# Two-block transformer on one core: columns spread by transposes in place of fp32 products, reciprocals written wide

## The chip, the cores and the metric

The kernel runs on one core of one Trainium2 chip (trn2). The metric is the device time of one execution in microseconds. One execution was also taken by the hardware profiler; all rows below come from it.

## The reference

Two transformer blocks follow each other on x (1, 512, 1024), all in fp32. Only what matters for the change is shown.

```python
def rms_norm(x, gain):
    y = xf * lax.rsqrt(jnp.mean(xf * xf, axis=-1, keepdims=True) + NORM_EPS)
    return (y * gain.astype(jnp.float32)).astype(x.dtype)

def first_block(x, c, ...):
    cond = jax.nn.silu(c)
    for i in range(DEPTH):                       # 2 layers
        mod = (cond @ ada_w[i] + ada_b[i]).reshape(b_, N_SUBLAYERS, 3, D_MODEL)
        h = adaln(x, norm_g[i, 0], mod[:, 0, 0], mod[:, 0, 1])
        x = x + 0.5 * (1.0 + mod[:, 0, 2]) * swiglu(h, ...)
        # mixer: pooling in layer 0, fox_attention (16 heads of 64) in layer 1
        # a second swiglu with its own adaln
def second_block(x, ...):
    # layer 0: hybrid attention. Heads 0-7 attend through masks that count three dilations;
    # 4 more head pairs are differential: softmax 1 minus lam * softmax 2, then an rms norm
    # layer 1: gated linear recurrence; each layer ends with a convolutional feed-forward
```

In both attentions every softmax row is divided by its sum.

## The kernel before

**Layout.** X, HH and HL hold activations with the 1024 channels on the partitions, as 8 tiles of 128 x 512 tokens. All large products are fp32 made of three fp32r products: each weight chunk of 128 x 1024 (raw) is loaded by SyncE, split by ScalarE into a high part wh (L543) and by VectorE into a low part wl (L998), and TensorE multiplies wh by the high and low parts of the activation and wl by the high part (L1732, L1921, L1786 to L1789). Four chunks are in the ring. Each engine has one fixed order of work, written by hand; semaphores join them. The two PSUM halves PS[0] and PS[1] have four banks each.

**Norms.** There are ten (six adaln in the first block, four in the second). VectorE adds squares per tile, `square_sums` (L1812) sums them over the partitions, so that the mean square stands as a column of tokens: st4[:, 1, a] holds the roots of 128 tokens. `spread_root` (L1851 to L1860) turns a column into a row and repeats it on all partitions: an fp32 product of the column, stretched to 128x128 by a broadcast, with the identity. The product shows as two records. Nine norms make two calls (one per half of the tokens) with two products each, the first norm makes one call with four. The calls stand between the large products: in `tilewise` behind the 11th block of the second half, in `halved_units` behind the third tile, in the pooling stage and at the start. `h_scale` on VectorE (L1152) waits for rb_ready, which the call signals. `keep_busy` (L1803) runs five bf16 products behind the first call.

**Condition.** At the start (L2018) eight such products spread silu(c) over PS[1]; VectorE copies the result to condb (L1341), against which it multiplies the rows of ada_w (L1068). Then TensorE transposes x (L2027).

**Attention.** Both attentions go by pairs of heads, 8 pairs each. For pair i the steps are: `score_mms` (L1935), on VectorE `pair_scores` (L1277: score plus bias, with the row minimum as a by-product), on ScalarE `pair_exp` (L658, with the sums Z[:, slot, qt]), on VectorE `pair_sums` (L1282 to L1295, reciprocal into rz), `transposes` of the probabilities (L1987, 20 blocks in five rounds through banks 4, 5, 6, 7, 4), `turned_copies` by ScalarE (L670) and VectorE (L1306), `value_mms` (L1940 to L1967), and the multiplication by the spread reciprocals (L1548) into OT; then the split of the result into HH (ScalarE L849) and HL (VectorE L1573). The stages of three pairs overlap: in iteration i of the loop TensorE makes the scores of pair i, the values of pair i-2 and the transposes of pair i-1. Third round of the transposes: it waits for pv_read of the pair before, which L1548 signals, because both use bank 6.

Only "plain" pairs spread their reciprocals: all 8 pairs of the first attention (fox) and the last 4 of the second (i >= COMBINED = 4), twelve in all. `value_mms` makes 8 products (L1950), four blocks of tokens times two heads, each with 64 stretched columns, into bank 7; ScalarE copies that to OT (L836). In the differential pairs (the first 4 of the second attention) L1289 to L1295 combine the two heads instead, and L1552 and L1561 scale.

The order on VectorE in iteration i of the first attention is: scores of rounds 0 and 1 of pair i, pair_sums of pair i-1, L1548 of pair i-2, scores of round 2, three copies L1306, L1573. On ScalarE: exponentials of round 0, L836, exponentials of round 1, L670 twice with the exponentials of round 2 behind, L849. pair_exp waits for rz_ready of the pair two before (its Z slot), value_mms for rz_ready of its own pair. QB holds the queries; tile i of it is read by score_mms of pair i alone.

Of the kernel before, what the change touches and what calls it, by code (L numbers as in the profile page):

```python
# [179 lines left out]
def build(nc, A, out, upto=None):  # L180
    plan, NCH = make_plan(upto)
    ctx = ExitStack()
    with ctx:
# [32 lines left out]
        ident = sb("ident", [128, 128])  # L216
# [7 lines left out]
        st4 = sb("st4", [128, 6, 4])  # L224
# [4 lines left out]
        Z = sb("Z", [128, 4, 4])  # L229
        rz = sb("rz", [128, 4, 4])  # L230
# [3 lines left out]
        QB = arena[:, 0:4096].rearrange("p (k t) -> p k t", k=KT)  # L234
# [44 lines left out]
        PS = [ctx.enter_context(nc.psum_tensor(f"PS{i}", [128, 4, 512], F32)) for i in range(2)]  # L279

        def plain(fox, i):

            return fox or i >= COMBINED

        def tile_of(fox, i):

            return i if fox else SECOND[i]
# [6 lines left out]
        def t_rounds(fox, i):  # L294

            if i == 0:
                return T_AHEAD[fox]
            return T_FIRST if fox else T_PLAIN if plain(fox, i) else T_COMBINED

        def attend_bank(b, g):  # L300

            return PS[(g + b // 4) % 2][:, b % 4, :]
# [47 lines left out]
        bias_masked, rz_ready, combined, sub_summed, rz_spread, rz_copied = (sem(n) for n in (  # L350
            "bias_masked", "rz_ready", "combined", "sub_summed", "rz_spread", "rz_copied"))
# [35 lines left out]
        def P(name, i=0, n=1):  # L387
            c = COL[name] + i
            return par[:, c:c + n]
# [594 lines left out]
        def _(dve):  # L984
# [297 lines left out]
            def pair_sums(pair, i, fox):  # L1282

                slot = 2 * (pair % 2)
                dve.wait_ge(p_ready, 8 * pair + 8)
                if plain(fox, i):
                    nc.vector.reciprocal(rz[:, slot:slot + 2, :], Z[:, slot:slot + 2, :]).then_inc(rz_ready, 1)
                    return
                link(nc.vector.reciprocal(rz[:, slot:slot + 2, :], Z[:, slot:slot + 2, :]))  # L1289
                link(TS(rz[:, slot + 1, :], rz[:, slot + 1, :], lam[:, 5:6], None, ALU.mult))  # L1290
                TT(rz[:, slot + 1, :], rz[:, slot + 1, :], Z[:, slot, :], ALU.mult).then_inc(rz_ready, 1)
                dve.wait_ge(rz_ready, pair + 1)
                for qt in (3, 2, 1, 0):
                    first, second = (SP_[:, slot + u, SEG[qt]:SEG[qt + 1]] for u in range(2))
                    STT(first, second, rz[:, slot + 1, qt:qt + 1], first, ALU.mult, ALU.add).then_inc(combined, 1)  # L1295
# [38 lines left out]
            for st in plan:  # L1334
                kind, c, g = st["kind"], st["c"], st["g"]
# [59 lines left out]
                elif kind == "ffn":  # L1395
# [4 lines left out]
                    for ng, nt in st["halves"]:  # L1400
                        if ada:
                            paired = st is plan[2] and c == st["c"]
                            if paired:
# [5 lines left out]
                                e, cv, g, c, j = e + 2, cv + 2, g + 2, c + 8, j + 2  # L1409
                            for u in range(2 if paired else 0, ng):  # L1410
# [5 lines left out]
                                e, cv, g, c, j = e + 1, cv + 1, g + 1, c + 4, j + 1  # L1416
# [11 lines left out]
                        e, cv, g, c, j = e + 2 * pairs, cv + 2 * pairs, g + 2 * pairs, c + 8 * pairs, j + 2 * pairs  # L1428
                        if ng % 2 and not ada:
                            split_until(c + 4 + RING)  # L1430
                            hidden_group(st, e, g, cv, j, 4 * pairs, 0)
                            e, cv, g, c, j = e + 1, cv + 1, g + 1, c + 4, j + 1
# [36 lines left out]
                elif kind == "attproj":  # L1469
                    for i in range(4):  # L1470
                        c += 4
                        if st["fox"] and i == 0:
# [7 lines left out]
                            m, p, mn = accf[0:HEADS, 5120:5632], SG[0:HEADS, 0, :], PR[0:HEADS, 0, :]  # L1480
# [13 lines left out]
                        q = st["q"] + i  # L1494
# [5 lines left out]
                        for p in range(2):  # L1500
# [4 lines left out]
                            y, t = PR[:, :, :], WK[:, 2 * p:2 * p + 2, :]  # L1505
# [12 lines left out]
                    pair, fox = st["a"] // 2, st["fox"]  # L1518
# [13 lines left out]
                elif kind == "attend":  # L1532
                    p0, fox = st["a"] // 2, st["fox"]
                    for i in range(2, PAIRS + 2):
# [10 lines left out]
                        if plain(fox, i - 2):  # L1545
                            o = OT_flat(b)
# [147 lines left out]
                elif kind == "finish":  # L1694
                    for a in range(4):
                        dve.wait_ge(out_act, a + 1)
                        dve.wait_ge(tile_done, st["td"] + a + 1)
                        o = XOUT[:, a, 512:D]
# [4 lines left out]
        def _(pe):  # L1703
            MM = nc.tensor.matmul
# [146 lines left out]
            def spread_root(nm, h):  # L1851


                ps, halves = PS[nm["g"] % 2], (h,) if nm["n"] else (0, 1)
                pe.wait_ge(root_ready, norm_at(nm, h))
                for a in (a for half in halves for a in (2 * half, 2 * half + 1)):
                    o = 128 * (a % 2)
                    mm = MM(ps[:, 2 + a // 2, o:o + 128], st4[:, 1, a:a + 1].broadcast_to((128, 128)), ident[:, :],
                            start=True, stop=True, skip_group_check=True)
                mm.then_inc(rb_ready, 1)  # L1860

            def turn_back(g, half):
# [77 lines left out]
            def value_mms(pair, i, fox, g):  # L1940

                bank, slot, col = attend_bank(6, g), 2 * (pair % 2), 128 * tile_of(fox, i)
                pe.wait_ge(pt_act, before(pair + 1, 2, 2))
                if plain(fox, i):
                    pe.wait_ge(rz_ready, pair + 1)
                    if not fox:
                        pe.wait_ge(pt_vec, before(pair, 3, 1) + 2)
                    for qt in range(4):
                        for u in range(2):
                            mm = MM(attend_bank(7, g)[64 * u:64 * u + 64, 128 * qt:128 * qt + 128],  # L1950
                                    rz[:, slot + u, qt:qt + 1].broadcast_to((128, 64)), ident[:, :],
                                    start=True, stop=True, skip_group_check=True)
                    mm.then_inc(rz_spread, 1)
                pe.wait_ge(pt_vec, before(pair + 1, 3, 1))
                if plain(fox, i):
                    for kt in range(4):
                        for u in range(2):
                            at_, n = 10 * u + KT_AT[kt], 4 - kt
                            mm = MM(bank[64 * u:64 * u + 64, 128 * kt:512], VB[:, kt, col + 64 * u:col + 64 * u + 64],
                               PTS[:, at_:at_ + n, :].rearrange("p n q -> p (n q)"), start=(kt == 0), stop=(kt == 3),  # L1960
                               skip_group_check=True)
                else:
                    for qt in range(4):
                        for kt in range(qt + 1):
                            mm = MM(bank[:, 128 * qt:128 * qt + 128], PTS[:, KT_AT[kt] + qt - kt, :], VB[:, kt, col:col + 128],
                                    start=(kt == 0), stop=(kt == qt), skip_group_check=True)
                mm.then_inc(pv_done, 1)  # L1967
# [41 lines left out]
            for st in plan:  # L2009
                kind, c, g, n = st["kind"], st["c"], st["g"], st["n"]  # L2010
                h_ready_at = lambda k: [(h_ready, st["h"] - KT + k + 1)]
                nm = plan[plan.index(st) - 1] if kind in ("ffn", "attproj", "rec", "poolmix") else None
                if kind == "start":
                    pe.wait_ge(ident_in, 16)
                    pe.wait_ge(cond_act, 1)
                    for i in range(KT):
                        o = 128 * (i % 4)
                        mm = MM(PS[1][:, 2 + i // 4, o:o + 128], P("cond", i).broadcast_to((128, 128)), ident[:, :],  # L2018
                                start=True, stop=True, skip_group_check=True)
                    mm.then_inc(cond_wide, 1)  # L2020
                    for k in range(KT):
                        if k % 4 == 0:
# [14 lines left out]
                elif kind == "ffn":  # L2037
                    e = st["e"]
                    c_last = c + sum(4 * ng + nt for ng, nt in st["halves"])
                    for ng, nt in st["halves"]:  # L2040
                        pairs, e2 = ng // 2, e
                        if nm:
# [5 lines left out]
                            c, g, e2, pairs, nm = c + 8, g + 2, e2 + 2, pairs - 1, None  # L2048
# [7 lines left out]
                        for half in range(2):  # L2056
# [6 lines left out]
                            c, g = c + nt // 2, g + 1  # L2063
# [331 lines left out]
```

## Time and profile before

| | us |
|---|---|
| median of 3 runs | 2970.56 (2969.76 to 2972.46) |
| profiled execution, its time | 2972.09 |
| profiled execution, its span | 2970.2 |
| TensorE busy | 2934.7, 99% |
| VectorE busy | 1648.1, 55% |
| ScalarE busy | 1144.9, 39% |
| GpSimd busy | 145.5, 5% |

The span goes from the first to the last instruction. Matmul ends are modelled by the profiler; the starts of successive records tell how long a group holds TensorE. An idle time in brackets at the end of a timeline row is that of the engine before the instruction, with the instruction that ended it.

### The profile page before, as it was taken

The page shows a single profiled execution, that of the slowest core. Times are in us where ns is not written, and L with a number is a line of the kernel's source. Part 1 is how long each engine was busy: PE and PEld are TensorE (multiplying, and loading weights), DVE is VectorE, ACT ScalarE, POOL GpSimd, SP SyncE. Part 2 cuts the span into 40 slices and gives each one's busy share as a digit, 9 for nine tenths or more (in the row PEclk, how much of TensorE's full clock was granted, in tenths as well). Part 3 has the DMA queues.
Part 4 walks back from the last instruction along what each step waited for, and adds up shares of the span by engine and source line. Part 5 has one row for each costly group of instructions (what it writes and reads, how often), then busy time and mean ns, then how long its engine had stood idle before and what let it go on. Part 6 is the DMA issues. An engine that isn't in the chain of part 4 may idle for free. (4 is left out here: it accounts for less than half of the span.)

```text
span 2970.2 us, 37552 instructions
## 1 busy us (share of the span) xinstructions
PE 2934.7 (99%) x14365; PEld 2443.0 (82%) x14365; DVE 1648.1 (55%) x2338; ACT 1144.9 (39%) x1586; POOL 145.5 (5%) x297
## 2 busy tenths in 40 slices
PE   9999989999999999999999999999999999999999
PEld 7888888888888888868888888768888888888887
DVE  7747476444653336875433357766535557754453
ACT  4223253222432225464332234554423338443242
POOL 0101001000010001040000000110000001000000
PEclk9999999999999999999999999999999999999999
DMA  7837326554362322241322223422322322323222
GB/s 295 275 127 262 121 73 227 175 163 149 123 218 93 99 99 97 92 168 68 114 94 98 99 74 100 141 88 86 101 98 92 100 92 79 107 85 106 92 99 71
DMA packets 100914, 366.56 MB, mean 123 GB/s; under 512 B 11248, under 2 KB 11808, under 8 KB 100784
## 3 DMA queue, kind: packets, MB, share of 16 engines
q1 hardware_dynamic: 77616, 276.56, 27.4%
q0 software_dynamic: 23168, 88.17, 8.8%
q8 instruction: 93, 1.52, 0.2%
q14 instruction: 37, 0.30, 0.0%
HBM read 362.51 MB, written 2.18 MB: 123 GB/s over the span
## 5 line engine op out<-in xcount | busy, mean ns | idle before, releaser
L998 DVE TENSOR_TENSOR wl<-raw,wh 128x1024 fp32r<-128x1024 f32 x501 | 609.2, 1225 | 971.9 <-ACT wh L543 971.8
L543 ACT ACTIVATE wh<-raw 128x1024 fp32r<-128x1024 f32 x501 | 524.1, 1056 | 1205.4 <-PE PS L1732 1148.7
L1732 PE MATMUL PS<-HH,wh 128*128 128x512 f32 x2432 | 947.6, 390 | 4.8 <-DVE HL L1580 3.2
L1732 PE MATMUL PS<-HL,wh 128*128 128x512 f32 x2432 | 947.0, 389 | 0.0
L1732 PE MATMUL PS<-HH,wl 128*128 128x512 f32 x2432 | 946.6, 389 | 0.0
L1732 PEld LDWEIGHTS PS<-HH,wh 128*128 128x128 f32 x2432 | 456.8, 188 | 101.9 <-DVE HL L1580 4.3
L1732 PEld LDWEIGHTS PS<-HH,wl 128*128 128x128 f32 x2432 | 456.9, 188 | 95.1
L1732 PEld LDWEIGHTS PS<-HL,wh 128*128 128x128 f32 x2432 | 456.9, 188 | 94.3
L1732 PE MATMUL PS<-AH,wh 128*128 128x512 f32 x848 | 330.1, 389 | 0.5 <-DVEq L1615 0.5
L1732 PE MATMUL PS<-AH,wl 128*128 128x512 f32 x848 | 329.9, 389 | 0.0
L1732 PE MATMUL PS<-AL,wh 128*128 128x512 f32 x848 | 329.9, 389 | 0.0
L1732 PEld LDWEIGHTS PS<-AH,wh 128*128 128x128 f32 x848 | 159.2, 188 | 34.3 <-DVEq L1615 0.9
L1732 PEld LDWEIGHTS PS<-AH,wl 128*128 128x128 f32 x848 | 159.2, 188 | 33.0
L1732 PEld LDWEIGHTS PS<-AL,wh 128*128 128x128 f32 x848 | 159.2, 188 | 33.0
L1332 DVE TENSOR_TENSOR AL<-PR,AH 128x1024 fp32r<-128x1024 f32 (+1 forms) x68 | 83.3, 1226 | 87.4 <-ACT AH L694 87.4
L1322 DVE SCALAR_TENSOR_TENSOR WK<-PS,par,WK 128x511 f32<-128x511 f32 (+1 forms) x192 | 128.1, 740 | 0.0
L694 ACT ACTIVATE AH<-PR 128x1024 f32 (+1 forms) x68 | 72.1, 1061 | 137.3 <-DVE PR L1313 103.5
L1068 DVE CUSTOM_DVE_ANT_0 acc<-acc 128x1024 f32<-128x1024 f32 x86 | 104.1, 1219 | 5.1 <-DMA acc<-in_stream 5.0
L1921 PE MATMUL PS<-AH,wh 128*128 128x256 f32 (+1 forms) x312 | 100.1, 321 | 0.0
L1921 PE MATMUL PS<-AL,wh 128*128 128x256 f32 (+1 forms) x312 | 99.3, 318 | 0.0
L1921 PE MATMUL PS<-AH,wl 128*128 128x256 f32 (+1 forms) x312 | 99.3, 318 | 0.0
L658 ACT ACTIVATE acc<-acc,NM 128x128 f32<-128x128 f32 (+3 forms) x128 | 70.5, 553 | 32.6 <-DVE NM L1277 32.5
(278 smaller groups left out, 3117.7 us busy)
## 6 DMA issues: line engine op xcount, KB each, us to landing
raw<-in_stream SPq DMA_DIRECT2D x501, 512.0 KB, 3.3
acc<-in_stream POOLq DMA_DIRECT2D x86, 512.0 KB, 4.8
piece<-in_stream POOLq DMA_DIRECT2D x42, 512.0 KB, 4.8
arena<-in_stream SPq DMA_DIRECT2D x16, 512.0 KB, 12.5
TBa<-negcum POOLq DMA_DIRECT2D x8, 640.0 KB, 5.1
TBa<-in_alibi POOLq DMA_DIRECT2D x8, 640.0 KB, 4.7
TBb<-negcum POOLq DMA_DIRECT2D x4, 640.0 KB, 4.9
piece<-negcum POOLq DMA_DIRECT2D x4, 640.0 KB, 6.0
```

The source lines that it names most:

```text
L543: F(wh[:, r, :], raw[:, r, :], ACT.Copy).then_inc(hi_done, 1)
L658: F(seg, seg, ACT.Exp, bias=NM[:, slot, qt:qt + 1], scale=-1.0, accum_out=Z[:, slot, qt:qt + 1]).then_inc(p_ready, 1)
L694: F(dst, PR[:, :, :], ACT.Copy).then_inc(act_hi, 1)
L998: TT(wl[:, r, :], raw[:, r, :], wh[:, r, :].bitcast(F32), ALU.subtract).then_inc(lo_done, 1)
L1068: return nc.vector.tensor_tensor_reduce(tile, tile, condb, 1.0, 0.0, ALU.mult, ALU.add, mod[:, s, j:j + 1])
L1322: ins = STT(y, PS[g % 2][:, t, 0:S - sh], w, y, ALU.mult, ALU.add)
L1332: TT(dst, PR[:, :, :], hi.bitcast(F32), ALU.subtract).then_inc(a_ready, 1)
L1732: mm = MM(PS[g % 2][:, j, :], l, x, start=(first and i == 0), stop=(last and i == 2), skip_group_check=after_halves)
L1921: mm = MM(PS[g % 2][:, t, cols(h)], l, x, start=(k == 0 and i == 0), stop=(k == nt - 1 and i == 2), skip_group_check=True)
```

## The change

Three places that spread a column by an fp32 product with the identity now do it by a transpose of the same stretched column: spread_root, the condition, and the reciprocals in value_mms. For the last, the eight products of 64 columns become four transposes of 128: the reciprocals of a pair are first written out stretched. VectorE's reciprocal in pair_sums of a plain pair reads the 8 sums of a token 64 times each and writes 128x512 into tile tile_of(fox, i) of QB, the query tile that the pair no longer needs, where it wrote 128x8 into rz. Semaphores and their counts stay as they are, and so does the order of instructions on every engine. Differential pairs are untouched.

```diff
+        def rz_wide(fox, i):
+            return QB[:, tile_of(fox, i), :]
@@ pair_sums (VectorE)
                 if plain(fox, i):
-                    nc.vector.reciprocal(rz[:, slot:slot + 2, :], Z[:, slot:slot + 2, :]).then_inc(rz_ready, 1)
+                    nc.vector.reciprocal(rz_wide(fox, i).rearrange("p (q u f) -> p u q f", q=4, u=2),
+                                         Z[:, slot:slot + 2, :].unsqueeze(3).broadcast_to((128, 2, 4, 64)))\
+                        .then_inc(rz_ready, 1)
                     return
@@ spread_root (TensorE)
                     o = 128 * (a % 2)
-                    mm = MM(ps[:, 2 + a // 2, o:o + 128], st4[:, 1, a:a + 1].broadcast_to((128, 128)), ident[:, :],
-                            start=True, stop=True, skip_group_check=True)
+                    mm = nc.tensor.transpose(ps[:, 2 + a // 2, o:o + 128], st4[:, 1, a:a + 1].broadcast_to((128, 128)),
+                                             ident[:, :])
@@ value_mms (TensorE)
                     for qt in range(4):
-                        for u in range(2):
-                            mm = MM(attend_bank(7, g)[64 * u:64 * u + 64, 128 * qt:128 * qt + 128],
-                                    rz[:, slot + u, qt:qt + 1].broadcast_to((128, 64)), ident[:, :],
-                                    start=True, stop=True, skip_group_check=True)
+                        t = slice(128 * qt, 128 * qt + 128)
+                        mm = nc.tensor.transpose(attend_bank(7, g)[:, t], rz_wide(fox, i)[:, t], ident[:, :])
@@ start (TensorE)
                         o = 128 * (i % 4)
-                        mm = MM(PS[1][:, 2 + i // 4, o:o + 128], P("cond", i).broadcast_to((128, 128)), ident[:, :],
-                                start=True, stop=True, skip_group_check=True)
+                        mm = nc.tensor.transpose(PS[1][:, 2 + i // 4, o:o + 128], P("cond", i).broadcast_to((128, 128)),
+                                                 ident[:, :])
```

## Rows read from the trace of the kernel before

**Rows 1.** The page: span, and busy time, share and instructions of each engine.

```profile
span 2970.2 us, 37552 instructions
PE 2934.7 (99%) x14365; PEld 2443.0 (82%) x14365; DVE 1648.1 (55%) x2338; ACT 1144.9 (39%) x1586; POOL 145.5 (5%) x297
```

**Rows 2.** Busy time by windows, both attentions; columns: stretch, length, engines, PEclk, DMA.

```profile
1290.00:1320.00 30.00, 30.00 (x240) 20.81 (x239) 22.80 (x69) 21.15 (x59) 14.52 (x31) 1.00 0.45 150
...
1920.00:1950.00 30.00, 25.48 (x172) 17.15 (x171) 23.44 (x79) 23.99 (x95) 14.64 (x54) 0.95 0.48 170
```

**Rows 3.** Instructions of one line: count, ns min/median/max, starts, shape.

```profile
L1858 PE MATMUL PS<-ident,st x80: 270/275/421, 13.3 to 2574.7; 128*128 128x128 f32 x80
...
L1950 PE MATMUL PS<-ident,rz x192: 272/273/323, 1298.2 to 1973.3; 128*64 128x128 f32 x192
```

**Rows 4.** Timeline of TensorE around one root call; columns: start us, us, what.

```profile
1138.70 0.28 PE L1921 MATMUL PS<-AH,wl 128*128 128x256 f32 x1
...
1138.82 0.60 PE L1858 MATMUL PS<-ident,st 128*128 128x128 f32 x4
...
1139.18 0.36 PE L1921 MATMUL PS<-AH,wh 128*128 128x256 f32 x1
```

**Rows 5.** Timeline of TensorE: 20 transposes and the product behind them.

```profile
1291.24 2.34 PE L1987 MATMUL PS<-ident,acc 128*128 128x128 f32 x20
...
1293.35 0.48 PE L1732 MATMUL PS<-wh,HH 128*128 128x512 f32 x1
```

**Rows 6.** VectorE's groups by line and shape: count, busy us, mean ns, idle before.

```profile
L1306 DVE COPY PTS<-PS 128x512 f32<-128x512 f32 x36 | 23.4, 687 | 5.6 <-PE PS L1987 4.9
...
L1516 DVE COPY arena<-PS 128x2048 f32<-128x2048 f32 x2 | 4.6, 2283 | 0.0
...
L1287 DVE RECIPROCAL rz<-Z 128x8 f32<-128x8 f32 x12 | 2.4, 197 | 0.0
...
L1044 DVE TENSOR_SCALAR gains<-par 128x1 f32<-128x1 f32 x7 | 0.5, 145 | 0.0
...
L1230 DVE TENSOR_TENSOR mod<-mod,par 128x8 f32<-128x8 f32 x1 | 0.2, 168 | 0.0
```

**Rows 7.** Timeline of all engines: a round of the first attention, the next reciprocal.

```profile
1304.01 0.60 ACT L670 ACTIVATE PTS<-PS 128x512 f32<-128x512 f32 x1 [0.65 <-PE PS L1987]
...
1305.49 0.62 ACT L849 ACTIVATE HH<-acc 128x512 fp32r<-128x512 f32 x1
...
1306.13 0.69 DVE L1573 TENSOR_TENSOR HL<-acc,HH 128x512 fp32r<-128x512 f32 x1 [1.00 <-ACT HH L849]
...
1306.27 1.09 PE L1950 MATMUL PS<-ident,rz 128*64 128x128 f32 x16
...
1306.74 0.28 DVE L1277 CUSTOM_DVE_ANT_0 acc<-PS,TBa 128x128 f32<-128x128 f32 x1
...
1307.19 2.32 PE L1959 MATMUL PS<-PTS,arena 128*64 128x512 f32 x16
...
1309.34 0.20 DVE L1287 RECIPROCAL rz<-Z 128x8 f32<-128x8 f32 x1
...
1309.83 0.69 DVE L1548 TENSOR_TENSOR acc<-PS,acc 128x512 f32<-128x512 f32 x1 [0.28 <-ACT acc L836]
...
1317.41 0.20 DVE L1287 RECIPROCAL rz<-Z 128x8 f32<-128x8 f32 x1
```

**Rows 8.** Timeline of VectorE in the second attention: reciprocal and what follows.

```profile
1943.12 0.20 DVE L1287 RECIPROCAL rz<-Z 128x8 f32<-128x8 f32 x1
1943.67 0.69 DVE L1552 TENSOR_TENSOR acc<-PS,rz 128x512 f32<-128x512 f32 x1 [0.35 <-PE PS L1965]
...
1969.47 0.69 DVE L1548 TENSOR_TENSOR acc<-PS,acc 128x512 f32<-128x512 f32 x1 [1.13 <-PE PS L1959]
```

**Rows 9.** The start: the condition's line, and a window (columns as in rows 2).

```profile
L2018 PE MATMUL PS<-ident,par x16: 421/421/580, 3.4 to 6.7; 128*128 128x128 f32 x16
...
19.00:21.00 2.00, 2.00 (x6) 1.54 (x6) 2.00 (x4) 0.23 (x1) 0.00 (x0) 0.50 1.03 412
```

## The prediction

> **What bounds the kernel now.** I read the page first: over a span of 2970.2 us TensorE is busy 99% of the time, VectorE 55% [rows 1]. So a microsecond taken from TensorE is normally a microsecond of the result, and one given to VectorE normally costs nothing. That average must not be used for the two attention stages, so next I read the table by windows. In 30 us of the first attention TensorE is busy 30.0, VectorE 22.8 and ScalarE 21.2 us; in 30 us of the second TensorE falls to 25.5, and the granted clock there to 0.95 [rows 2]. There three engines hand one pair of heads round, and a slower VectorE can set the pace. The third view is the timeline of one round, the fourth the groups by line and shape.
>
> **Part 1, the roots (spread_root, L1858).** One fp32 product shows as two records: 40 products, 80 records [rows 3]. A call in the middle of the stream makes two products; its four records hold TensorE from 1138.82 to 1139.18, 0.36 us [rows 4]. An fp32 transpose is one record: 20 of them take 1291.24 to 1293.35, 0.105 us each [rows 5]. Two take 0.21, so a call saves 0.15 us. There are 18 such calls, two in each of nine norms, nearly all of them with TensorE work back to back on both sides: **2.7 us saved**. The reader of the root, VectorE's L1152, gets it 0.15 us sooner as well, and no transfer hangs on it. A transpose that reads one column 128 times is not in the trace. From below it can't cost less than the 0.09 us of one product record [rows 4], from above the two records that it replaces; I take 0.105, the ordinary transpose, because its row has the same shape and type. Bounds 0 to 3.2 us saved.
>
> **Part 2, the condition (L2018).** Eight products, 16 records, run before x has landed, and the first transposes of x wait for that DMA anyway, so the saving is worth nothing. Their records take 421 ns where the same shape later takes 270 to 275: TensorE runs at half speed there although the granted clock reads 1.00 [rows 3, 9]. Half as many records leave TensorE idle before x lands, so the 32 transposes of x can stay at the slow pace longer. At worst they take about 3 us more; part of this is covered, because the root, which is spread behind them, comes from VectorE later than they end. The stretch from 19 to 21 us runs at a granted 0.50 (1.2 GHz) [rows 9]; such a fall of about 3.4 us costs 1.7 us and can move or double. I take +0.5 us, bounds -1.5 to +4.
>
> The Trainium skill, page "TensorE: Matmul & The Clock Gate", Part 4, says that transpose mode doesn't count as busy for the clock. By that rule products turned into transposes make falls of the clock likelier, at 1.7 us each as above. The trace does not bear it out in the first attention, where half of the instructions are transposes and the clock stays at 1.00 [rows 2].
>
> **Part 3, the products of the reciprocals (L1950).** Eight products with 64 columns each, 16 records, from 1306.27 to the next group's 1307.19, 0.92 us [rows 7]; four full transposes take 0.42 [rows 5], with a changeover 0.5. It saves 0.4 us a pair, twelve pairs, **if TensorE sets the pace there**.
>
> **Part 4, the reciprocal (L1287).** It wrote 8 elements a partition and now writes 512, on VectorE, in order, ahead of L1548. This decides the case. An 8-element reciprocal takes 197 ns. An 8-element product of two tensors takes 168. Copies take 687 ns for 512 elements and 2283 for 2048: 1.04 ns an element on a base of 155 [rows 6]. Two readings of 197 are possible. Either the reciprocal has a longer start and then runs at 1.04 ns an element: 512 elements take 0.72 us. Or each element takes longer: (197 - 168) / 8 + 1.04 = 4.7 ns, or on the copies' base (197 - 155) / 8 = 5.2 ns, or on the base of a one-element operation, 145 [rows 6], 6.5 ns. That makes 2.6, 2.8 or 3.5 us for 512. A division in several steps is the more natural reading of a row that stands 17% above another operation of its size, and I take 2.8 us, on the copies' base, since a reciprocal has one operand like them. Ends: 0.72 and 3.5 us.
>
> The Trainium skill, page "VectorE: DVE Perf Modes", the walkthrough's hardware budget, describes the reciprocal as an iterative divide with a repeat count of 8. Eight steps of 1.04 ns would be 4.4 us for 512 elements. The same rule gives 222 ns for 8 elements, and the row has 197, so in size the trace agrees only in part.
>
> Now the place. In a round of the first attention the order on VectorE is L1573, six score reductions, reciprocal, L1548, two more reductions, three copies. The rounds are 8.07 us apart (1309.34 and 1317.41), and from the reciprocal's start to L1548's are 0.49 us, the last 0.28 waiting for ScalarE's L836 [rows 7]. An instruction starts some 0.08 us before the end of the one ahead of it (L1573 takes 0.69, the next starts after 0.61 [rows 7]), so a reciprocal of 2.8 moves L1548 to 2.72 us behind its start, 2.23 later. What follows L1548 today takes 3.68 us until L1573. It starts with the third round of transposes, which waits for L1548 to free its bank, then ScalarE's copy L670, two exponentials and L849 [rows 7]. With TensorE waiting at that bank this part shrinks to 8 x 0.105 for two rounds of transposes + 0.28 for the end of the last record [rows 3] + 0.5 + 1.0 (together 1304.01 to 1305.49) + 0.64 for L849 and the start behind it = 3.3 us. The round becomes 3.3 + 0.61 + 2.60 + 2.72 + 0.69 = 9.9 us, **1.85 us longer**, and TensorE has over 2 us of idle in it, so that part 3 is worth nothing. Five rounds: 9.25. In the first round the cover is 0.99, +1.73; in the last with a reciprocal 1.21, +1.51. Pair 0's reciprocal stands among weight splits with free time on all engines: 0. In the second attention four reciprocals are wide; L1552 or L1548 starts 0.55, 1.30, 1.31 and 1.33 us behind them (the first stands whole in [rows 8], of the last its idle time; the covers of the rounds not shown, six in all, are read in the same way), so +2.17, +1.42, +1.41 and +1.39. Together **18.9 us**. Each 0.1 us on the reciprocal moves it by 1.1 us: 16.5 with 2.6 us and 26.6 with 3.5. I know of no wait that moves: the bank of L1950 and ScalarE's first exponential wait for a reciprocal that is a whole round old.
>
> The gaps of 2 us in TensorE invite falls of the clock inside the attentions. Most of a fall is hidden by those same gaps; one that runs into the dense products behind costs 1.7 us. I take +1, bounds 0 to 5.
>
> **Sum.** -2.7 + 0.5 + 0 + 18.9 + 1.0 = +17.7 us. The profiled execution has a span of 2970.2 and took 2972.1, so 1.9 lie around the span; its time after is 2989.8. It stands 1.5 above the median of 2970.56, so the prediction is 2988.3, **2988 us**, +0.6%.
>
> **Rivals.** (a) *The reciprocal only has a longer start*, 0.72 us. Then L1548 comes 0.15 us later than today at most, the pace stays TensorE's, and part 3 counts: about 0.3 us in each of eleven rounds, 3.3 us, and 2.7 from the roots: -6, 2965 us. This is the other side. It decides as long as the reciprocal's start-to-start time stays under about 0.9 us, the cover it has in a round; for it speaks that a single size can't tell start from rate. (b) *Eight steps an element*, 4.4 us: 11 x 1.6 = 17.6 us more than my sum, 3006 us; against it speaks the 197 ns. That is the price of the page's rule, worked out from the copies' 1.04 ns. (c) *The reciprocal is iterative but half as slow, about 1.7 us*, part start and part rate: 18.9 - 12.1 = 6.8, in all +5.6, 2976 us. (d) The change would not do what it says if stretched columns slowed the transposes to the price of products: part 1 goes, 2.7 us more than the sum; inside the range.
>
> **How the numbers follow.** Chances: forecast with 2.6 to 3.5 us a reciprocal 0.63 (its own range 2981 to 2998), (a) 0.13, (b) 0.19, (c) 0.05. The range 2975 to 3008 takes in (b) and (c) and leaves (a) out. A measurement of this kernel can tell about 0.2%, 6 us. Slower by more is the forecast, (b) and a part of (c): 0.85. Within 0.2%: half of (a), the rest of (c): 0.08. Faster: half of (a): 0.07.
>
> **What would show it.** The row of the wide reciprocal, 128x512, at 2.6 to 3.5 us is the step on which all rests; at 0.7 rival (a) has won. The time from one such row to the next in the first attention should be 9.9 instead of 8.07 us; TensorE's transposes should wait for L1548, some 2 us a round. The root's call should take 0.21 us instead of 0.36, with half as many records. The number of stretches at 0.50 should rise by no more than three. The prediction is wrong if the reciprocal's rate is wrong, or if the second attention hides more than its covers say.

## The result and the profile after

The change made the kernel slower, by the mechanism that was forecast and by a little more than the forecast size:

| | before | after |
|---|---|---|
| median of 5 runs, us | 2972.03 | 2995.69 |
| lowest to highest, us | 2969.76 to 2972.70 | 2992.21 to 2996.92 |
| profiled execution: time, span, us | 2972.1, 2970.2 | 2995.9, 2994.0 |
| mean granted clock | 0.997 | 0.994 |

The ratio of after to before is 1.0076, with a 95% interval of 1.0065 to 1.0086. The forecast was 2988, with a range of 2975 to 3008. (The 2970.56 that it starts from is the median of the first three of the five runs before.)

In the code after the change the line numbers are higher by 4 to 6: the reciprocal is L1291 (was L1287), the accumulation behind it L1554 (L1548), the turning transposes L1991 (L1987), the copies behind them L674 and L1312 (L670, L1306), the spread of the reciprocals L1956 (L1950), that of the roots L1864 (L1858), the split behind the round L1579 (L1573).

The page after, which answers to [rows 1]:

```profile
span 2994.0 us, 37168 instructions
PE 2934.9 (98%) x14173; PEld 2437.1 (81%) x14173; DVE 1683.1 (56%) x2338; ACT 1144.6 (38%) x1586; POOL 144.1 (5%) x297
```

TensorE has 192 records fewer and is busy for the same 2935 us; VectorE has as many instructions as before and is busy for 35.0 us more. Twelve rows account for all of it and a little more. VectorE's groups by line and shape (count, busy us, mean ns, idle before), beside which [rows 6] has 12 at 197 ns:

```profile
L1291 DVE RECIPROCAL arena<-Z 128x512 f32<-128x512 f32 x12 | 40.2, 3348 | 0.0
L1295 DVE RECIPROCAL rz<-Z 128x8 f32<-128x8 f32 x4 | 0.8, 198 | 0.0
```

Twelve reciprocals grew from 2.4 to 40.2 us, 37.8 more. The span grew by 23.8. So most of the time added to an engine that is busy 56% of the span became time of the kernel. The waits of TensorE say how (who waited, for whom: us in total, times, longest):

```profile
PE PS L1991 <- DVE acc L1554: 19.3, 10, 2.4
PE PS L1991 <- DVE acc L1558: 3.1, 4, 0.9
```

The transposes at L1991 want the bank that L1554 reads, and L1554 stands behind the reciprocal on VectorE. One round of the first attention, from the timeline of all engines (start us, us, what, and in brackets the idle time and what ended it), to be laid beside [rows 7]:

```profile
1299.74 3.35 DVE L1291 RECIPROCAL arena<-Z 128x512 f32<-128x512 f32 x1
...
1303.01 0.63 DVE L1554 TENSOR_TENSOR acc<-PS,acc 128x512 f32<-128x512 f32 x1
...
1303.69 1.53 PE L1991 MATMUL PS<-ident,acc 128*128 128x128 f32 x12 [1.64 <-DVE acc L1554]
...
1306.94 0.69 DVE L1579 TENSOR_TENSOR HL<-acc,HH 128x512 fp32r<-128x512 f32 x1 [0.83 <-ACT HH L853]
...
1307.55 0.28 DVE L1281 CUSTOM_DVE_ANT_0 acc<-PS,TBa 128x128 f32<-128x128 f32 x1
...
1310.15 3.35 DVE L1291 RECIPROCAL arena<-Z 128x512 f32<-128x512 f32 x1
...
1313.42 0.63 DVE L1554 TENSOR_TENSOR acc<-PS,acc 128x512 f32<-128x512 f32 x1
...
1314.10 2.15 PE L1991 MATMUL PS<-ident,acc 128*128 128x128 f32 x12 [2.40 <-DVE acc L1554]
```

From one reciprocal to the next are 10.41 us, where [rows 7] have 8.07. The round can be added up from these rows: 3.27 from the reciprocal's start to L1554's, 0.63 for L1554, 3.30 from its end to L1579, 0.61 until the score reductions begin, 2.60 for these. That is 10.41.

Where the 23.8 us arose, from the starts of the same instructions in both traces:

| stretch | before, us | after, us | difference |
|---|---|---|---|
| start to the first reciprocal | 1283.65 | 1282.21 | -1.4 |
| first attention, to its last L1554 (before: L1548) | 70.50 | 88.79 | +18.3 |
| on to the first reciprocal of the second attention | 545.62 | 544.69 | -0.9 |
| second attention, to its last L1554 | 75.96 | 85.28 | +9.3 |
| on to the end of the span | 994.5 | 993.0 | -1.4 |

### The profile page after: what moved, and what is told of

Same layout as the page of the kernel before. It is cut to its first block and busy times, and to the rows that moved or that the text cites. A ratio compares the mean times of both kernels' runs of the same rounds, so it can differ in the third digit from the quotient of the medians.

```text
span 2994.0 us, 37168 instructions
## 1 busy us (share of the span) xinstructions
PE 2934.9 (98%) x14173; PEld 2437.1 (81%) x14173; DVE 1683.1 (56%) x2338; ACT 1144.6 (38%) x1586; POOL 144.1 (5%) x297
## 6 DMA issues: line engine op xcount, KB each, us to landing
arena<-in_stream SPq DMA_DIRECT2D x16, 512.0 KB, 12.6
```

## The experiments

Each kernel ran beside the kernel before. In this table the ratio to before has its 95% interval behind it; the change is in us against the runs of before that go with it.

| kernel | median, us | ratio | against before |
|---|---|---|---|
| the change | 2995.69 | 1.0076 (1.0065 to 1.0086) | +23.7 |
| roots and condition only | 2969.28 | 0.9989 (0.9980 to 0.9998) | -3.3 |
| roots only | 2968.84 | 0.9986 (0.9977 to 0.9995) | -3.7 |
| wide reciprocal and its transposes only | 2996.91 | 1.0082 (1.0067 to 1.0098) | +24.4 |
| half of the wide reciprocal | 2973.20 | 1.0003 (0.9993 to 1.0012) | +1.1 |
| wide reciprocal, products kept | 2992.59 | 1.0071 (1.0057 to 1.0085) | +20.7 |
| wide reciprocal later in the round | 3002.75 | 1.0101 (1.0086 to 1.0117) | +30.6 |
| small reciprocal, VectorE spreads it | 2966.34 | 0.9978 (0.9968 to 0.9987) | -6.2 |
| the same, later in the round | 2967.68 | 0.9985 (0.9976 to 0.9994) | -4.4 |
| small reciprocal, ScalarE spreads it | 2967.47 | 0.9984 (0.9975 to 0.9993) | -4.7 |

**The parts alone.** The first kernel is the one before with the transposes for roots and condition, the second has them for the roots alone, the third is the change with both put back:

```diff
-                    mm = MM(ps[:, 2 + a // 2, o:o + 128], st4[:, 1, a:a + 1].broadcast_to((128, 128)), ident[:, :],
-                            start=True, stop=True, skip_group_check=True)
+                    mm = nc.tensor.transpose(ps[:, 2 + a // 2, o:o + 128], st4[:, 1, a:a + 1].broadcast_to((128, 128)),
+                                             ident[:, :])
```

> Only the roots and the condition are spread by transposes; the attentions are as before. Theory A (the changed kernel's trace: a call holds TensorE 0.13 us, from 1137.73 to 1137.86, against 0.36 before): 18 calls x 0.23 = 4.1 us less, the start about 0.2 us later, so 3.9 us less than before. Theory B (the recorded sum, 0.105 us a transpose): 2.7 us less. Theory C (it does nothing, time is lost again in waits): 0.

> Only the roots are spread by transposes. Theory A (the condition's products are hidden behind the load of x): the same time as with the condition changed too, within 0.5 us, so 4.1 us less than before. Rival (fewer records at the start leave TensorE slow for longer): 0.5 to 4 us less time than with both changed.

> Only the wide reciprocals with their transposes; roots and condition as before. Theory A (all of the loss comes from the 3.35 us reciprocal ahead of the product with the spread reciprocals): about 27.6 us more than before, 18.3 in the first attention and 9.3 in the second. Rival (part of the loss comes from the start or the roots): less than 26 us more.

Measured: -3.3 us for roots and condition, -3.7 us for the roots alone, so the condition gives and takes nothing that can be seen. Theories A (3.9) and B (2.7) of the first kernel can't be told apart by its 3.3; the row of the root call, shown further below, does that. For the wide reciprocal with its transposes it is +24.4 us, where theory A had 27.6 and the rival less than 26. So theory A missed by 3, but not for the rival's reason: by the same five stretches as in the table above, this kernel differs from the one before by -0.6, +15.6, 0.0, +8.9 and -0.7 us, and all of its loss, 24.5 us, is in the attentions. What it lacks of the 27.6 is 2.7 us in the first attention, and there its trace differs from the change's in the clock. Its rounds are all 10.41 us; the change has two of 10.88 and 11.29, and a last stretch that is 1.3 us longer, each with a fall of the clock in it (an interval at the lower level, 0.50 of full speed). Over the same 30 us, the change first and then this kernel (stretch, length, engines, granted clock, DMA):

```profile
1290.00:1320.00 30.00, 25.96 (x165) 16.91 (x165) 25.34 (x58) 18.10 (x51) 9.62 (x21) 0.94 0.41 146
1290.00:1320.00 30.00, 25.96 (x173) 16.79 (x173) 25.05 (x56) 18.61 (x53) 10.98 (x22) 1.00 0.39 134
```

The parts add up roughly: 24.4 - 3.3 = 21.1, beside the 23.7 measured. The intervals reach 3 to 5 us either way, and the 2.7 us of the clock are about the difference. The loss is in the attentions, where parts 3 and 4 are, and the small gain in part 1; the products put back, below, part 3 from 4.

**The size of the reciprocal.** Half of it, 256 elements in place of 512:

```diff
-                    nc.vector.reciprocal(rz_wide(fox, i).rearrange("p (q u f) -> p u q f", q=4, u=2),
-                                         Z[:, slot:slot + 2, :].unsqueeze(3).broadcast_to((128, 2, 4, 64)))\
+                    nc.vector.reciprocal(rz_wide(fox, i)[:, 0:256].rearrange("p (q u f) -> p u q f", q=2, u=2),
+                                         Z[:, slot:slot + 2, 0:2].unsqueeze(3).broadcast_to((128, 2, 2, 64)))\
```

> The changed kernel with the wide reciprocal over the first two of four token blocks alone (128x256); the reciprocals of the other two blocks are left out, so their results are not the reference's. Theory A (the cost is a rate, 6.25 ns an element, and a round of the attention lengthens by what the reciprocal takes beyond its cover): the row takes 0.147 + 256 x 6.25 = 1.75 us, 1.6 less than in the changed kernel, and eleven rounds give back 17 to 18 us: about 10 us above the kernel with narrow reciprocals and copy, 2976 to 2979. Rival (a long start that grows little with size): the row stays above 2.5 us and the time above 2985.

Measured: 2973.2 us, 22.5 below the change. VectorE's group and, in the fence behind it, TensorE's wait in this kernel:

```profile
L1291 DVE RECIPROCAL arena<-Z 128x256 f32<-128x256 f32 x12 | 21.0, 1748 | 0.0
```

```profile
PE PS L1991 <- DVE acc L1554: 5.0, 9, 0.8
```

The row is as expected, 1.75 us. With it the sum of a round is 1.67 + 0.63 + 3.30 + 0.61 + 2.60 = 8.81 us, and all five rounds of the first attention are 8.81 us apart in the trace. The reciprocal is then 1.6 us shorter, and the kernel 22.5 us: 11 x 1.6 is 17.6. The time undercut the expected 2976 to 2979 by 2.8 us or more. Most of the rest is the clock: in the first attention this kernel keeps 1.00, the change has 0.95. Its attentions take 74.28 and 78.12 us. Beside the kernel with the wide reciprocal and its transposes alone, whose rounds in the first attention no fall of the clock lengthened (86.10 and 84.82 us), the half size gives back 11.8 + 6.7 = 18.5 us, near the 17.6; beside the change itself 14.5 + 7.2 = 21.7.

**The products put back.** The wide reciprocal stays, the eight products of 64 columns return:

```diff
-                        t = slice(128 * qt, 128 * qt + 128)
-                        mm = nc.tensor.transpose(attend_bank(7, g)[:, t], rz_wide(fox, i)[:, t], ident[:, :])
+                        for u in range(2):
+                            o = 128 * qt + 64 * u
+                            mm = MM(attend_bank(7, g)[64 * u:64 * u + 64, 128 * qt:128 * qt + 128],
+                                    rz_wide(fox, i)[:, o:o + 64], ident[:, :],
+                                    start=True, stop=True, skip_group_check=True)
```

> The changed kernel with its wide reciprocal and its roots, but the eight fp32 products of 64 columns a pair back in place of the four transposes; they read the wide columns, so everything that is computed is the reference's. It measures part 3 alone, while VectorE sets the pace. My step 'part 3 is worth nothing once the reciprocal is wide' expects the time of the changed kernel, 2995.7 us within 1.5, rounds of the first attention of 10.4 us as there, and TensorE's wait at L1991 for VectorE's L1554 shorter by about the 0.5 us a round that the products take longer. Rival: TensorE's work in a round still counts in full, 0.4 to 0.5 us in each of eleven rounds, about 5 us more, 3000 to 3001 us.

Measured: 2992.6 us (2991.8 to 2994.6). The median is 3.1 below the change, the runs overlap with the change's 2992.2 to 2996.9, and it is nowhere near 3000; but the expected 2995.7 within 1.5 was missed too, on the fast side. Its wait (L1991 is L1994 here), and two reciprocals of its timeline:

```profile
PE PS L1994 <- DVE acc L1554: 15.9, 10, 2.1
```

```profile
1298.35 3.35 DVE L1291 RECIPROCAL arena<-Z 128x512 f32<-128x512 f32 x1
1308.76 3.35 DVE L1291 RECIPROCAL arena<-Z 128x512 f32<-128x512 f32 x1
```

TensorE does more and waits 3.4 us less over ten waits. Three of the five rounds are 10.41 us as in the change; the two others, with a fall of the clock in them, are 10.57 and 10.95 where the change has 10.88 and 11.29. So in these rounds an instruction taken from TensorE only lengthens its wait: part 3 is worth nothing beside the wide reciprocal. That the median is even lower goes with the clock. By windows (stretch, length, engines, granted clock, DMA), first the change, then this kernel:

```profile
1270.00:1380.00 110.00, 94.39 (x556) 61.88 (x557) 86.19 (x184) 59.92 (x166) 31.84 (x70) 0.95 0.35 121
1900.00:2010.00 110.00, 93.94 (x546) 64.52 (x545) 83.41 (x206) 64.75 (x196) 20.11 (x70) 0.95 0.31 113
```

```profile
1270.00:1380.00 110.00, 97.00 (x658) 66.07 (x655) 85.36 (x182) 59.95 (x167) 32.32 (x70) 0.97 0.35 122
1900.00:2010.00 110.00, 94.64 (x597) 65.53 (x597) 80.36 (x204) 63.22 (x195) 19.14 (x68) 0.97 0.32 116
```

The time spent at 0.50 is twice what is missing to 1.00: 11 us in each attention of the change, 6.6 us here, 8.8 us less in all. At the level of 1.2 GHz the dense work takes double, so up to half of that, 4.4 us, is lost time. The spans of the two traces differ by 4.1 us: 1.7 in the first attention, 0.5 in the second, 1.4 ahead of the first reciprocal (in the first 30 us the change has a clock of 0.94, this kernel 1.00) and 0.5 behind the attentions. That is an accounting from one trace of each; no run holds the clock apart, and whether the products themselves keep it up is taken up below.

**The reciprocal's place.** The wide reciprocal moved behind the last scores of the round, ahead of the copies L1312 instead of ahead of L1554:

```diff
-                        if i <= PAIRS and plain(fox, i - 1):
-                            pair_sums(p0 + i - 1, i - 1, fox)
...
                             pair_scores(p0 + i, i, fox, g, (2,))
+                        if i <= PAIRS and plain(fox, i - 1):
+                            pair_sums(p0 + i - 1, i - 1, fox)
```

> The changed kernel with the full wide reciprocal, but behind the product with the spread reciprocals (L1554) and the scores of the last round, so ahead of the three copies. Theory A (with 3.3 us more a round VectorE has more work than a round is long, so the place gives back only its waits): the rounds become 9.7 us instead of 10.4 to 10.9, the time 4 to 8 us less than the changed kernel's, about 2990. Rival (only the place ahead of L1554, where TensorE waits for a bank, costs time): the rounds go back to 8.1 us and the time to about 2968.

Measured: 3002.8 us, 7 above the change, where 5 below was expected. This was a miss. TensorE's waits in this kernel, and behind them the longest in the timeline of the second attention:

```profile
PE PS L1991 <- DVE PTS L1312: 13.4, 4, 3.9
PE PS L1963 <- DVE PTS L1312: 7.1, 7, 1.0
PE PS L1956 <- DVE arena L1291: 5.0, 6, 2.3
```

```profile
1963.23 3.35 DVE L1291 RECIPROCAL arena<-Z 128x512 f32<-128x512 f32 x1
...
1967.69 1.28 DVE L1312 COPY PTS<-PS 128x512 f32<-128x512 f32 x2
...
1968.43 1.11 PE L1991 MATMUL PS<-ident,acc 128*128 128x128 f32 x4 [3.93 <-DVE PTS L1312]
```

L1554 is free now, and the next thing behind the reciprocal is late instead: the copies that empty the banks for the next transposes, by up to 3.9 us. In the first attention the rounds came down only from 10.41 to about 10.15, and the one behind them went from 7.8 up to 10.3; in the second they went from 9.1, 12.6, 11.4, 11.4 and 9.0 us to 10.3, 15.9, 15.0, 14.1 and 10.5. My reason had looked at one wait and not at what comes to stand behind the moved instruction. VectorE is the pace of the round, and at both places that were tried something that TensorE wants stands behind the reciprocal. The clock is not what makes the 7 us: three of the four executions took 3002.0 to 3003.1 us at a mean clock of 0.994, that of the change. The profiled one is the fourth, 3006.5 us at 0.992, so the rounds of its second attention, where the clock is 0.88, are somewhat too long for the median.

**A short way to the same columns.** The reciprocal of 8 elements as before, and a copy that repeats it into 512:

```diff
-                    nc.vector.reciprocal(rz_wide(fox, i).rearrange("p (q u f) -> p u q f", q=4, u=2),
-                                         Z[:, slot:slot + 2, :].unsqueeze(3).broadcast_to((128, 2, 4, 64)))\
+                    link(nc.vector.reciprocal(rz[:, slot:slot + 2, :], Z[:, slot:slot + 2, :]))
+                    nc.vector.tensor_copy(rz_wide(fox, i).rearrange("p (q u f) -> p u q f", q=4, u=2),
+                                          rz[:, slot:slot + 2, :].unsqueeze(3).broadcast_to((128, 2, 4, 64)))\
```

> The changed kernel, but VectorE takes the reciprocals of 8 elements (0.20 us) and then copies them stretched to 128x512. Theory A (it is the length of the reciprocal, 6.25 ns an element, not the writing of 512 elements or the transposes of QB): the copy takes 0.43 to 0.69 us, the product L1548 comes 0.2 to 0.4 us later than before in a round, the rounds are within 7.7 to 8.1 us, and the time is 4 to 7 us less than before. Rival (the wide write, the transposes from QB or the order cost the time): the rounds stay above 9 us and the kernel stays more than 10 us slower than before.

Measured: 2966.3 us, 6.2 below the kernel before and 29 below the change; the ratio's interval lies below 1, and this median is the lowest of all kernels here. Its groups on VectorE, and the same instructions in the timeline of one round:

```profile
L1292 DVE COPY arena<-rz 128x512 f32<-128x512 f32 x12 | 5.5, 460 | 0.4
L1291 DVE RECIPROCAL rz<-Z 128x8 f32<-128x8 f32 x12 | 2.4, 197 | 0.0
```

```profile
1307.16 0.20 DVE L1291 RECIPROCAL rz<-Z 128x8 f32<-128x8 f32 x1
1307.39 0.58 DVE L1292 COPY arena<-rz 128x512 f32<-128x512 f32 x1
1307.89 0.68 DVE L1555 TENSOR_TENSOR acc<-PS,acc 128x512 f32<-128x512 f32 x1
```

L1555 (the accumulation, one line further down here) starts 0.73 us behind the reciprocal, inside the 0.9 us of cover that the prediction found. TensorE is busy in all 30.0 us of the first attention's window again, at a clock of 1.00, and the rounds are 7.8 to 8.0 us behind a first of 8.55 (before: 8.07 behind 8.84). Parts 1 and 3 then both count: 3.3 to 3.7 for the roots, and 2.5 to 2.9 more for the transposes of the reciprocals. The stretches of the trace say the same: the first attention is 1.7 us shorter than before, the second 0.9. Four transposes hold TensorE for 0.59 us, from 1312.01 to 1312.60, where the products of [rows 7] hold it for 0.92:

```profile
1312.01 0.66 PE L1957 MATMUL PS<-ident,arena 128*128 128x128 f32 x4
1312.60 1.73 PE L1964 MATMUL PS<-PTS,arena 128*64 128x512 f32 x8
```

Two variants ask whether the spread can be made cheaper still: the same pair of instructions later in the round, as in the experiment on the place, and the copy on ScalarE, ahead of its first copy L674, with a semaphore of its own for TensorE.

> Narrow reciprocals and VectorE's stretched copy, both behind L1555 and the last scores instead of ahead of L1555. Theory A (0.47 us of copy ahead of L1555 still holds the transposes of the third round a little): the rounds shrink from 7.8 to 7.6 us, the time by 1 to 2 us against the kernel with the copy ahead. Rival (TensorE is the pace already): no change within 1 us.

> Narrow reciprocals on VectorE; ScalarE writes them stretched to 128x512 ahead of its copies L674; TensorE transposes as in the changed kernel. Theory A (TensorE sets the pace once nothing sits on VectorE's chain; what is left is part 3's saving): the rounds are 7.6 to 7.8 us and the time within 2 us of the kernel with VectorE's copy. Rival (ScalarE's 0.5 us on its own chain of exponentials lengthens the round): rounds of 8.1 us or more, time 3 us or more above the kernel with VectorE's copy.

Measured: 2967.7 and 2967.5 us, both within 1.4 us of 2966.3 and neither better; beside their own runs of before they save 1.5 to 1.8 us less, inside the intervals. The rounds with the later copy are 7.8 to 7.9 us behind the first of 8.3; with ScalarE's, which takes 0.62 us there in place of VectorE's 0.46, they are 8.0 to 8.2. The later copy did not shorten the rounds to 7.6 as expected. ScalarE's missed its 7.6 to 7.8 and came near the rival's 8.1, without the rival's 3 us. In the traces the first attention takes 68.8 us with the copy ahead, 69.1 with the later one and 70.1 with ScalarE's. Once VectorE's part is inside its cover, TensorE is the pace, and the place of the copy is worth 1 to 2 us at most.

## Why the prediction was right, and where its sizes were off

**What sets the pace.** That the share of 55% on the page must not be used for the attentions was right, and it is the step that carried the sign. 37.8 us more on VectorE cost 27.6 us inside the attentions, 24.5 where the clock stayed up in the rounds. The rule of the round is that it lasts from the reciprocal's start to that of the accumulation, plus a fixed remainder. The prediction had 7.20 us for the remainder, the change's rows have 7.14; with this the half-size kernel should have rounds of 8.81 us, and it has.

**Part 4, the reciprocal's duration.** This is the term that was mis-sized. The prediction took 2.8 us, on the copies' base of 155 ns; the row reads 3.35. The slope between 8 and 512 elements is (3348 - 197) / 504 = 6.25 ns an element, between 256 and 512 (3348 - 1748) / 256 = 6.25 too, so it is a straight line with a base of 197 - 8 x 6.25 = 147 ns: the base of the one-element operation of [rows 6], 145 ns. The prediction had this line as its upper end, 3.5 us. One 8-element row carries the base and the rate together, and 10 ns on the base are 0.6 us at 512 elements. (By the prediction's own 1.1 us for each 0.1 us, a reciprocal of 2.6 us gives 16.7 and not 16.5.) With 3.35 the prediction's own formula gives 9.9 + (3.27 - 2.72) = 10.45 us a round and 18.9 + 11 x 0.55 = 24.9 us in all; its round was right in every other part.

The Trainium skill, page "VectorE: DVE Perf Modes", hardware budget, has the reciprocal as an iterative divide with a repeat count of 8. The rows agree in that an element costs several times a copy's, but 6.25 ns are six of the copies' 1.04 ns and not eight; 4.4 us and 3006 are refuted.

**The attentions' sums.** For the 24.9 us the trace of the change has 27.6: 18.3 in the first attention, where the formula with 3.35 gives 16.3, and 9.3 in the second, where it gives 8.6. Of the 2.0 us in the first, 1.3 are two rounds of 10.88 and 11.29 us in which the clock fell (the others are 10.41), and 0.7 is the round of pair 0, which the prediction had at 0 and the trace has at 17.53 for 16.85 us. The rest is two differences that nearly cancel: the last stretch grew by 3.0 us instead of 2.1, with a fall of the clock in it, and the first round grew by 0.7 less than reckoned. The kernel with the wide reciprocal and its transposes alone, where no fall lengthened a round of the first attention, has 15.6 + 8.9 = 24.5 us. So the formula was right to within half a microsecond once the reciprocal is put in as it is, and 2.7 of the 3 us above it are falls of the clock in the first attention.

**The clock.** The prediction allowed one fall's worth, 1 us, and at most three more stretches at 0.50. There are five more: three in the first attention and three stretches' worth in the second, where the trace before had one. Windows around them in the change, which have a clock of 1.00 in the trace before:

```profile
1314.00:1319.00 5.00, 4.90 (x24) 3.32 (x24) 3.88 (x12) 2.33 (x7) 1.09 (x2) 0.66 0.42 162
1334.00:1340.00 6.00, 4.60 (x24) 3.60 (x24) 4.41 (x10) 2.09 (x6) 1.09 (x2) 0.72 0.40 112
1364.00:1371.00 7.00, 6.03 (x32) 3.32 (x32) 3.43 (x6) 1.71 (x3) 0.00 (x0) 0.76 0.00 0
```

Ahead of these falls TensorE waited 1.6 to 2.4 us a round, round after round. In the kernels whose waits for L1554 are under a microsecond (half size) or gone (small reciprocal) the first attention keeps 1.00. But waits of that length don't bring a fall in every execution. The kernel with the wide reciprocal and its transposes alone waits just as long, as the line below shows, and has a single fall in the first attention, behind the five long rounds:

```profile
PE PS L1991 <- DVE acc L1554: 19.7, 10, 2.4
```

What decides whether a fall comes is open. Its price can be read, though: the three falls in the first attention of the change cost 2.7 us beside that kernel's one, 1.3 of them in the two lengthened rounds and 1.3 in the last stretch. The forecast had allowed 1.0 us for all.

The Trainium skill, page "TensorE: Matmul & The Clock Gate", Part 4, has transposes not counted as busy. The runs don't bear out that this matters here. The small reciprocal with all its transposes has the clock of the kernel before, 1.00 and 0.98 by the same two windows. Of the kernels with the wide reciprocal the one with the transposes alone has 0.98 and 0.95, the one with the products 0.97 and 0.97, the change 0.95 and 0.95: they differ as much among those with transposes as between transposes and products. The prediction's own argument against the rule rested on a wrong count: of the 72 records of a round of the first attention 20 are transposes, not half.

**Part 1, the roots.** Expected 2.7 us, measured 3.7 alone, and -3.8 us in the three stretches of the change outside the attentions. The intervals of the medians hold 2.7 too; it is the row that shows the term per call too small. TensorE's timeline at the call that [rows 4] show before:

```profile
1137.61 0.28 PE L1927 MATMUL PS<-AH,wl 128*128 128x256 f32 x1
1137.73 0.38 PE L1864 MATMUL PS<-ident,st 128*128 128x128 f32 x2
1137.86 0.36 PE L1927 MATMUL PS<-AH,wh 128*128 128x256 f32 x1
```

Two transposes of a stretched column hold TensorE for 0.13 us, from 1137.73 to 1137.86, and not for 0.21: 0.23 us saved in place of 0.15, and 18 x 0.23 = 4.1. The reason is not that such a transpose is quicker than an ordinary one. A narrower window shows the second one alone:

```profile
1137.84 0.27 PE L1864 MATMUL PS<-ident,st 128*128 128x128 f32 x1
```

It starts 0.11 us behind the first, and the next product only 0.02 to 0.03 us behind it. The last of the 20 ordinary transposes of [rows 5] stands as close to its successor, and the others start 0.11 us apart, as do the four product records of [rows 4], the last of them at 1139.15:

```profile
1293.32 0.27 PE L1987 MATMUL PS<-ident,acc 128*128 128x128 f32 x1
1293.35 0.48 PE L1732 MATMUL PS<-wh,HH 128*128 128x512 f32 x1
```

So a record of this shape costs 0.11 us where another one follows, whether ordinary transpose, stretched transpose or product, and the last of a group 0.03. The call lost two records of four at 0.11 each. The prediction's 0.105 and 0.09 are averages over groups of 20 and of 4 with that short last one in them, and can't be carried to a group of two; its lower bound of 0.09 was not a bound.

**Part 2, the condition.** Taken as +0.5 us for a clock that can move; roots with and without it differ by 0.4 us, inside the intervals. It still runs at 421 ns a record, as in [rows 9], before x is there.

**Part 3.** Nothing beside the wide reciprocal, as predicted, and shown by the products put back; 2.5 to 2.9 us beside a short one, where rival (a) had reckoned 3.3. The spread takes 0.33 us less of TensorE, against the 0.4 of the prediction.

**The rivals.** (a), a long start only, is refuted by the row: 3.35 us and not 0.72. But its time, 2965 us, and the point from which it decides, 0.9 us of cover, are what the small reciprocal with a copy does: 0.73 us, 2966.3. (b) falls with the six steps, (c), 1.7 us, with the same row; its time, 2976, can be laid beside the half-size kernel, 1.75 us and 2973.2. (d) fell too: stretched columns are transposed at the pace of ordinary ones, a record every 0.11 us.

The sum by measured terms, against the 23.8 us of the span: -3.8 outside the attentions, +27.6 inside.

## What to carry to other kernels

Read an engine's slack from one round and not from its share of the span: here an engine at 55% had 0.9 us of cover a round, and in the middle rounds nearly all above it was paid, 2.34 us of 2.40. Never widen the costly operation to get a wider layout; do it on the few elements and let a copy repeat them, here 0.20 + 0.46 us in place of 3.35. Where one short row is the only evidence for a rate, carry the line through the smallest row of the trace as well as through the likeliest, for a base that is off by ten nanoseconds is off by more than half a microsecond at 64 times the size.

## What the runs showed of the hardware

- A reciprocal on VectorE takes 147 ns and 6.25 ns an element a partition, on a straight line through 8, 256 and 512 elements; the 256 are four sums read 64 times each, the 512 eight. No run has 512 different inputs.
- A copy in SBUF of the same 512 repeated elements takes 0.46 us on VectorE (mean of 12, 0.43 in most) and 0.62 us on ScalarE. A copy of 512 elements out of PSUM takes 0.69 us on VectorE [rows 6], so the copies' 1.04 ns an element don't hold for this one.
- At full clock the starts of fp32 records of 128x128 follow each other at 0.11 us, be they transposes of different columns, transposes of one column read 128 times, or the records of a product; a product has two of them, a transpose one [rows 3 to 5]. The last record of a group is followed by the next product after 0.03 us, so a group of two shows 0.13 us and one of four 0.36.
- Falls of the clock in the first attention: none in the kernels with waits of TensorE below a microsecond a round; one to three in the kernels with waits of about two. The falls lengthened the first attention of the change by 2.7 us.
